# VectorE's chunk in a PEER decoder block: two drains a turn become semaphore waits, the coefficients are scaled behind the second row addition and asked for ahead of the rows

## The reference

```python
def peer_ffn(h, w_q, sk1, sk2, eu, ev):        # 512 tokens, D = 1024, 8 heads, 128 x 128 keys, top 16
    ...                                         # eidx: 128 experts a token, g: their softmax weights
    def chunk(args):
        ht, it, gt = args
        u = eu[it]
        a = jax.nn.gelu(jnp.einsum('ckd,cd->ck', u, ht).astype(jnp.float32), approximate=False) * gt
        return jnp.einsum('ck,ckd->cd', a.astype(ht.dtype), ev[it])
```

## Time and profile before

| | |
|---|---|
| median of 3 runs | 1521.03 us (1520.96 to 1522.51) |
| profiled execution, its own time | 1529.37 us |
| its span | 1527.6 us |
| granted TensorE clock, mean | 0.987 |
| TensorE busy | 1489.6 us (98%) |
| VectorE busy | 1333.8 us (87%) |
| GpSimd busy | 1028.9 us (67%) |

### The profile page before, as it was taken

How to read it: one execution, slowest core, us unless ns; L and a number is a source line. 1 busy time by engine, 2 the same in 40 slices (tenths; PEclk the granted TensorE clock), 3 DMA queues, 4 the chain that set the end, 5 groups by cost and what they waited for, 6 DMA issues and landing times.

```text
span 1527.6 us, 21852 instructions
## 1 busy us (share of the span) xinstructions
PE 1489.6 (98%) x7296; PEld 1236.3 (81%) x7296; DVE 1333.8 (87%) x2237; ACT 760.4 (50%) x1179; POOL 1028.9 (67%) x732
## 2 busy tenths in 40 slices
PE   7999999999999999999999999999999999999998
PEld 5887778888887888888878888888887888788886
DVE  6497666688998999989969999999999999999997
ACT  4644442433455555555455555454544555455553
POOL 6643224333886777778877777777777777777771
PEclk8999999899999999999999999999999999999999
DMA  9335447222776998989889999999999999999993
GB/s 361 98 104 173 154 149 266 79 83 83 220 237 191 284 293 278 293 278 315 285 299 396 396 389 401 370 377 393 393 388 360 380 398 395 368 390 395 396 404 129
DMA packets 219582, 444.58 MB, mean 291 GB/s; under 512 B 22360, under 2 KB 128984, under 8 KB 219232
## 3 DMA queue, kind: packets, MB, share of 16 engines
q1 hardware_dynamic: 174432, 309.04, 57.5%
q0 software_dynamic: 45056, 134.38, 23.1%
HBM read 407.68 MB, written 35.67 MB: 290 GB/s over the span
## 4 chain that ended last, share of the span: by engine, by line
PE 56%; POOL 27%; issue 8%; DMA 4%; DVE 3%; ACT 1%; DVEq 0%; SPq 0%; ACTq 0%; POOLq 0%
POOL coef L684 14%; POOL rows L678 13%; PE ps L1756 8%; PE ps L1757 8%; PE ps L1758 8%; PE ps L1505 4%; PE ps L1507 4%; PE ps L1506 4%; PE ps L1836 4%; PE ps L1805 2%; PE ps L1808 2%; PE ps L1811 2%; PE ps L1770 2%; PE ps L1838 2%; DMA coef<-gelu_spill,coef_at 2%
## 5 line engine op out<-in xcount | busy, mean ns | idle before, releaser
L635 POOL TENSOR_TENSOR wlo<-raw,whi 128x1024 fp32r<-128x1024 f32 x178 | 428.8, 2422 | 294.3 <-ACT whi L714 293.9
L1836 PE MATMUL ps<-acts,whi 128*128 128x512 f32 x1024 | 366.3, 397 | 0.0
L684 POOL DMA_INDIRECT coef<-gelu_spill,coef_at x256 | 299.5, 1170 | 82.0 <-issue 77.8
L678 POOL DMA_INDIRECT rows<-w_stream,row_at x256 | 273.0, 1067 | 78.0 <-issue 76.5
L1838 PE MATMUL ps<-acts,wlo 128*128 128x256 f32 x1024 | 287.3, 281 | 0.0
L714 ACT ACTIVATE whi<-raw 128x1024 fp32r<-128x1024 f32 x176 | 186.2, 1060 | 150.1 <-PE ps L1758 104.5
L1836 PEld LDWEIGHTS ps<-acts,whi 128*128 128x128 f32 x1024 | 192.7, 188 | 46.3
L1756 PE MATMUL ps<-whi,acts 128*128 128x512 f32 x512 | 200.7, 392 | 2.8 <-DVE gate_lo L1336 2.1
L1757 PE MATMUL ps<-wlo,acts 128*128 128x512 f32 x512 | 200.3, 391 | 0.0
L1758 PE MATMUL ps<-whi,acts 128*128 128x512 f32 x512 | 199.8, 390 | 0.0
L1838 PEld LDWEIGHTS ps<-acts,wlo 128*128 128x128 f32 x1024 | 193.6, 189 | 5.2
(11 more groups left out here) (253 smaller groups left out, 2582.8 us busy)
## 6 DMA issues: line engine op xcount, KB each, us to landing
raw<-w_stream SPq DMA_DIRECT2D x304, 512.0 KB, 5.4
values_in<-w_stream SPq DMA_DIRECT2D x128, 512.0 KB, 7.6
ada<-w_ada SPq DMA_DIRECT2D x32, 512.0 KB, 4.7
gelu_spill<-gout SPq DMA_DIRECT2D x64, 256.0 KB, 5.4
gate_spill<-gblock SPq DMA_DIRECT2D x8, 2048.0 KB, 10.4
gates<-gate_spill SPq DMA_DIRECT2D x32, 512.0 KB, 8.3
ada<-w_ada SPq DMA_DIRECT2D x32, 256.0 KB, 7.2
rows<-w_stream,row_at POOLq DMA_INDIRECT x256, 7.1
```

The lines of the kernel that those rows point to most:

```text
L635: g.tensor_tensor(wlo[:, s, :], raw[:, s, :], whi[:, s, :].bitcast(F32), ALU.subtract)\
L678: g.indirect_dma_start(rows[m % ROWS][:, :], None, w_front.rearrange("c p n -> (c p) n"), bass.IndirectOffsetOnAxis(row_at[:, t * P + n:t ...
L684: g.indirect_dma_start(coef[:, t, n:n + 1], None, gelu_dram.rearrange("t p g (e o) -> (t p g e) o", o=1), bass.IndirectOffsetOnAxis(coef_a ...
L1836: mm(ps[:, 6 + e % PAIRED, :].rearrange("p (n t) -> p n t", n=2), wh, acts[:, :, k, 0:HALF], start=k == 0, stop=False)
```

## The change

The drain at the start of a turn goes; in its place VectorE waits for two semaphores, one that its own row additions count (`row_added`, from the second turn on) and a new one that its scalings count (`coefs_scaled`). The drain behind a scaling goes too. The scaling of the next turns' coefficients moves from the start of a turn to the end of the chunk before, between the second row addition and `make_value_lo`. One drain is added ahead of the loop. GpSimd asks for the coefficients of turn `n + 1` before the rows of turn `n`, not behind them.

```diff
             for n in range(FIRST_ROWS, NK):
-                fetch_rows(n)
                 if n + FIRST_COEFS - FIRST_ROWS < NK:
                     fetch_coefs(n + FIRST_COEFS - FIRST_ROWS)
+                fetch_rows(n)
...
             def scale_coefs(b):
                 dve.wait_ge(coef_in[b % COEF_RING], 16 * PAIR * COEFS * (b // COEF_RING + 1))
                 some = slice(b * COEFS, (b + 1) * COEFS)
-                v.tensor_tensor(coef[:, :, some], coef[:, :, some], gate_of[:, :, some], ALU.mult)
-                dve.drain()
+                v.tensor_tensor(coef[:, :, some], coef[:, :, some], gate_of[:, :, some], ALU.mult).then_inc(coefs_scaled, 1)
 
             def add_row(n, t):
 
+                m = n * PAIR + t
                 if t == 0:
-                    dve.drain()
-                    if n % COEFS == 0:
-                        scale_coefs(n // COEFS)
-                m = n * PAIR + t
+                    if n >= 1:
+                        dve.wait_ge(row_added, m)
+                    dve.wait_ge(coefs_scaled, n // COEFS + 1)
...
             v.tensor_copy(gate_of[:, :, :].rearrange("p t n -> p (t n)"), fetched[2])
+            dve.drain()
             for e in range(NK):
                 due = [(n, t) for n in range(rows_done(e), rows_done(e + 1)) for t in range(PAIR)]
+                if e == BEHIND:
+                    scale_coefs(0)
...
                 for n, t in due[1:]:
                     add_row(n, t)
+                for n in range(max(1, rows_done(e + 1)), rows_done(e + 2)):
+                    if n % COEFS == 0:
+                        scale_coefs(n // COEFS)
                 if e + 1 < NK:
                     make_value_lo(e + 1)
```

More of the change, by code:

```diff
@@ L389, in build @@
         row_added = sem("row_added")
+        coefs_scaled = sem("coefs_scaled")
         turned = sem("turned")
```

## The result

The changed kernel takes 1572.81 us in the median (four runs, 1562.79 to 1583.73), the kernel before beside it 1521.77 us: a ratio of 1.0325, with a 95% interval of 1.025 to 1.0399. It is slower, as forecast, but by 51 us and not by 19, and outside the range of 1511 to 1560. The profiled execution took 1578.97 us, 49.6 more than that of before. Its runs also spread over 21 us, those of before beside them over 2, and the 29 runs of before taken beside experiments 13 to 15 over 11.

The account below looks back on a forecast made before the run. TensorE, busy 98%, was taken to bound the kernel, losing 14.3 us to waits in the last stage. -14.3 + 28.3 (starved requests) + 5.1 (clock) = +19.1 us, on a median of 1521.03: 1540 us, range 1511 to 1560.

Parts of the forecast that it names:

- Drains out: VectorE's turn start: L1448 to the next instruction 1.14 us, not 1.31; turn 5.33 us, not 5.51; waits cost nothing.
- Scaling moved: VectorE's scaling, moved and without its drain, adds about 0.07 us to a turn instead of 0.24.
- Coefficients first: GpSimd's request order: coefficients gain 1.2 us, rows lose 2.5; row lead falls from 11.4 to 8.9 us.
- What the drains gave GpSimd: Without VectorE's gaps GpSimd makes seven requests in two turns where eight are needed; eight take 12.26 us.
- the walk: Stepping GpSimd's request ready times through VectorE's turn: back to back, three requests fit a 5.33 us turn; four are needed.
- Price of it: Cost of starved requests over the 96 turns of the 93 chunks: between 0 and 56.6 us, middle 28.3 taken.
- Waits do open gaps: VectorE's row waits restore GpSimd's four requests, but the next turn without one loses a request again; hence 28.3 us.
- upper bound: No wait restores GpSimd's four requests: 96 x (6.13 - 5.54) = 56.6 us over the 93 chunks.
- starved throughout: Rival: waits for rows do not restore GpSimd's requests; +47.4 us, 1568 us, chance 0.12.
- At TensorE's pace: With VectorE idle 0.3 us before `prod`, four requests fit; loss begins at the first two-turn chunk, 960 us.
- 3 x 1.7 = 5.1 us: Clock loss from long TensorE stalls on three chunks with two turns, 1.7 us each.
- some 48 us: Sign in the profile after: TensorE's excess over the 93 chunks some 48 us instead of 14.

Follow-up runs that it names:

- experiments 13 to 15: 13: changed kernel, drain replacing the opening waits; 14: same, 4/5 turns asked ahead; 15: kernel before, coefficients first, 4/5 turns ahead. 1522.4, 1519.8, 1520.3 us.
- 1: Kernel before with both drains replaced by semaphore waits; scaling place and request order stay old: 1591.8 us, ratio 1.0457.
- 2: Changed kernel with a drain again ahead of the addition that opens each turn, beside the semaphore waits: 1523.8 us, ratio 1.0008.
- 7: Changed kernel with three requests a turn: block 1's coefficients not fetched, so part of the computation is left out: 1511.6 us, ratio 0.9921.
- 9: Changed kernel with a drain ahead of the opening addition of odd turns only: 1560.6 us, ratio 1.0226.
- 10: Changed kernel with a drain ahead of the opening addition of even turns only: 1532.5 us, ratio 1.0061.
- Run 11: Changed kernel, no drain in the turns, with 4 turns of rows and 5 of coefficients asked for ahead instead of 3 and 4: 1577.9 us, ratio 1.0365.
- run 5: Changed kernel with one drain a turn, ahead of `make_value_lo`: 1522.6 us, ratio 1.0006.
- 3: Changed kernel with the old order of GpSimd's requests, rows ahead of the next coefficients: 1576.8 us, ratio 1.0366.
- run 13: Changed kernel with a drain in place of the two semaphore waits at the start of a turn: 1522.4 us, ratio 0.9997.

## Why the prediction was right and wrong

**Right**, by its own steps. *Drains out*: L1448 to the opening addition is 1.14 us in the median where no row is waited for (798.73 to 799.86 in the lines above), the turn 5.33 us, and the waits cost nothing there. *Scaling moved*: 0.07 us to the next instruction in the median. *Coefficients first*: coefficients' waits fell (14.8 to 5.6 us), rows are late, and where nothing starves the lead of the rows is 9.0 us for 8.9. *What the drains gave GpSimd*: the walk's three requests for four, shown by 1, 2, 7 and above all by 9 and 10. The trace disagrees with the sentence of the Trainium skill that was weighed (VectorE: DVE Perf Modes, The DRAIN you can't avoid: chaining without semaphores does not skip the pipe's emptying), by 1.14 us against 1.31. The same section also says that a next instruction that is not held starts earlier, and with that the trace agrees; the prediction left it out.

**Wrong** is the term "Price of it", where I took the middle of 0 and 56.6 us, and with it two sentences under it and the clock. The 49.7 us of the profile (40.3 in the 93 chunks, 9.4 ahead of them) against the forecast 19.1:

- *The share.* "Waits do open gaps", so half: 28.3 us, and 33.4 with the clock. The 93 chunks lost 54.6 us, nearly all of the upper bound of 56.6: the waits for rows did not give GpSimd its fourth request back. The 61.8 us of these waits did less for the requests than the 17 us that one drain in each of 96 turns makes (0.18 us each). As I read it, a gap helps a request only where it falls ahead of the instruction that the request would meet: run 9, with its 64 drains at the wrong turns, gets back a quarter of the loss, run 10, with as many at the right ones, four fifths. Back to back the walk was also too kind: 2.7 requests a turn at 794 to 811 us, not 3, nor 3.5 with the scalings, because some requests miss handovers. Both together came out at 6.06 us a turn in the stage's mean (784.3 to 1553.8 us for 127 turns), near the upper bound's 6.13. The rival "starved throughout", which had 1568 us and a chance of 0.12, was the right one.
- *The beginning.* "At TensorE's pace ... the same walk gives four again, so the loss begins" at 960 us. But VectorE is not at TensorE's pace when the turns begin. It waits 5.1 us for the first coefficients (before, 5.2) and then runs back to back to catch up, which is the very case of three requests. 9.4 us were lost ahead of 960. Run 11 shows that a larger lead does not change it.
- *The clock.* "3 x 1.7 = 5.1 us" for three stalls. From 960 to 1550 us TensorE stood over 1 us ten times, and 17.1 us of full clock went. Seen from TensorE the 54.6 us are 35.2 us of waits for `phi`, these 17.1, and 2.3 in no wait that I listed. But the clock is no second cause to be added: the upper bound counts GpSimd's requests and holds whatever TensorE does meanwhile, and without any clock it is already 2.0 over what was lost. No run tells the clock's own part.

(54.6 - 33.4) + 9.4 = 30.6 us; with 19.1 that is the 49.7. The sign "some 48 us" for the excess of the 93 chunks was itself added up wrongly: by the prediction's own terms it is 28.3 + 5.1 = 33.4. It measured 54.6. That this comes near the "some 48 us" is luck.

Still open: why a request ready within 0.07 us behind `prod`'s start is sometimes held until the `acc` addition and sometimes let go at the first handover. Of 42 such requests in the changed kernel 18 took 2.6 to 2.7 us, 18 were let go at the first handover and 6 took 0.95, at distances that overlap; in run 5, 82 of 84 took 0.95. It was counted, not tested apart; what it adds to the price is therefore not separated from the rest.

## What to carry to other kernels

Before a drain is taken out because its engine has time to spare, look at who uses the gap: another engine's requests may get through only there, and whether they do is read by laying the two timelines side by side and walking one turn. If such a walk has margins of hundredths of a microsecond and no slack in its count (four fit, four are needed), price the upper bound, not the middle: here what was starved did not recover by the waits that it caused. And where a loss is added up from TensorE's stalls, the clock behind them comes on top (here 17.1 us behind 35.2); where it is reckoned from the pace of what starves it, the clock is already in it.

## What the runs showed of the hardware

A request of GpSimd's that meets an instruction of VectorE's with two SBUF inputs can pass more than one handover. In the changed kernel 15 requests made ready 0.00 to 0.07 us behind `prod`'s start ended 0.90 us after the `acc` addition had begun, 2.6 to 2.7 us in all, with L1419 and `plo` in between; in runs 3, 7 and 11 it was 22, 17 and 18. The Trainium skill (SBUF — State Buffer, SBUF: two separate sides) has the shared port pair as an exclusive lock that the loser waits for until the other's instruction is over; the single handovers agree (0.90 us behind each), these cases go beyond it.

Semaphore waits whose condition has been met cost VectorE nothing where no drain stands before them: L1448 to the opening addition with its three waits is 1.14 us, and so is L1419 to `plo` with its one. Behind a drain two waits more add 0.10 us (1.41 in run 2 against 1.31 in run 13).
